# First half of the experts' down product as three rounded products, and gathered rows in two buffers in place of four

## The reference

```python
def swiglu(x, w_gate, w_up, w_down):
    return (jax.nn.silu(x @ w_gate) * (x @ w_up)) @ w_down
...
    def block(args):
        tok, e = args
        return swiglu(h_pad[tok], w_gate[e], w_up[e], w_down[e])

    out = lax.map(block, (row_tok.reshape(n_blocks, MOE_BLOCK), blk_exp))
    out = out.reshape(n_rows, D) * row_w[:, None]
    return jax.ops.segment_sum(out, row_tok, num_segments=T + 1)[:T]
```

## Time and profile before

| | |
|---|---|
| median of 3 runs | 2048.01 us (2043.39 to 2048.45) |
| the profiled execution | 2049.21 us, span 2047.6 us |
| PE busy | 1928.1 us, 94% of the span |
| DVE busy | 1038.1 us, 51% |
| ACT busy | 874.1 us, 43% |
| POOL busy | 373.5 us, 18% |
| mean rate of all transfers | 195 GB/s over the span |

### The profile page before, as it was taken

One profiled execution on the slowest core, in us unless ns is written; L12 is line 12 of the kernel. 1 busy time (PEld: TensorE's weight loads), 2 busy tenths in 40 slices (PEclk: granted clock), 3 DMA queues, 4 the chain that ended last, 5 costly groups with the idle time before them and its releaser, 6 DMA issues. The chain is left out here.

```text
span 2047.6 us, 34503 instructions
## 1 busy us (share of the span) xinstructions
PE 1928.1 (94%) x10264; PEld 1495.0 (73%) x10265; DVE 1038.1 (51%) x1532; ACT 874.1 (43%) x1210; POOL 373.5 (18%) x337
## 2 busy tenths in 40 slices
PE   4999999899899999989789999999999999999995
PEld 3999999899788666755547777777777777777772
DVE  4113401166438335545426666666666666666665
ACT  5110111244212212221246666666666666666663
POOL 0100100111111000000212222232223222222220
PEclk9999999899899999999889999999999999999997
DMA  7211311111443665425069896999998888897964
GB/s 260 74 52 41 123 52 31 32 63 62 144 142 113 229 230 206 143 85 196 1 228 347 261 346 182 317 295 300 331 301 271 269 273 306 244 352 253 300 180 172
DMA packets 182101, 399.64 MB, mean 195 GB/s; under 512 B 22425, under 2 KB 87185, under 8 KB 182046
## 3 DMA queue, kind: packets, MB, share of 16 engines
q1 hardware_dynamic: 149166, 312.16, 42.5%
q0 software_dynamic: 31680, 82.49, 15.7%
q10 hardware_dynamic: 1200, 4.26, 0.6%
HBM read 351.27 MB, written 80.64 MB: 211 GB/s over the span
## 5 line engine op out<-in xcount | busy, mean ns | idle before, releaser
L2184 DVE TENSOR_TENSOR wexp_lo<-wexp,wexp_hi 128x2048 fp32r<-128x2048 f32 x190 | 426.9, 2288 | 91.3 <-ACT wexp_hi L2135 88.3
L2135 ACT ACTIVATE wexp_hi<-wexp 128x2048 fp32r x190 | 353.4, 1907 | 52.4 <-issue 49.4
L2111 PE MATMUL bank<-wexp_down,hTe 128*128 x736 | 330.6, 592 | 0.0
L2086 PE MATMUL bank<-wexp_hi,x_hi 128*128 128x512 f32 x744 | 300.5, 404 | 3.8 <-DVE wexp_lo L2184 3.8
L2086 PE MATMUL bank<-wexp_hi,x_lo 128*128 128x512 f32 x744 | 292.0, 393 | 0.0
L2086 PE MATMUL bank<-wexp_lo,x_hi 128*128 128x512 f32 x744 | 290.4, 390 | 0.0
L2059 POOL DMA_INDIRECT acc_d<-ob,ixs x92 | 153.7, 1670 | 615.8 <-DMA acc_d<-ob,ixs 441.9
L2111 PEld LDWEIGHTS bank<-wexp_down,hTe 128*128 128x128 f32 x736 | 139.1, 189 | 139.4 <-issue 132.3
L547 PE MATMUL bank<-hT_hi,w_hi 128*128 128x344 f32 x576 | 187.3, 325 | 7.3 <-DVEq L659 7.3
L547 PE MATMUL bank<-hT_hi,w_lo 128*128 128x344 f32 x576 | 185.1, 321 | 0.0
L547 PE MATMUL bank<-hT_lo,w_hi 128*128 128x344 f32 x576 | 184.6, 320 | 0.0
(11 more groups left out here) (357 smaller groups left out, 2988.7 us busy)
## 6 DMA issues: line engine op xcount, KB each, us to landing
wexp<-in_w_exp_gate SPq DMA_DIRECT2D x128, 512.0 KB
wexp<-in_w_exp_up SPq DMA_DIRECT2D x128, 512.0 KB
wexp_down<-in_w_exp_down SPq DMA_DIRECT2D x128, 512.0 KB
wada<-in_w_ada SPq DMA_DIRECT2D x12, 2048.0 KB, 10.9
w_raw<-in_w_in SPq DMA_DIRECT2D x44, 512.0 KB, 3.9
gates_d<-gst POOLq DMA_DIRECT2D x48, 172.0 KB, 2.1
gate<-gates_d SPq DMA_DIRECT2D x16, 516.0 KB, 5.8
xn<-in_x_prompt ACTq DMA_DIRECT2D x8, 512.0 KB, 8.3
```

What stands on the lines that cost most here:

```text
L2086: last = pe.matmul(banks[0][:].rearrange("p (g n) -> p g n", g=2), stat[:, b, k, :], mov[:, b, :, k * FF:(k + 1) * FF], start=(k == 0 and ...
L2111: last = pe.matmul(banks[4 + half][:], hT[:, f, :], wdn[:, bass.ds(slot, 1), f, half * 512:half * 512 + 512].rearrange("p a n -> p (a n)") ...
L2135: act.activation(w_hi[:, b, g, :], wexp[:, bass.ds(e & (RING - 1), 1), g, :].rearrange("p a n -> p (a n)"), ACT.Copy).then_inc(whi_ok, 1)
L2184: dve.tensor_tensor(w_lo[:, b, g, :], wexp[:, bass.ds(e & (RING - 1), 1), g, :].rearrange("p a n -> p (a n)"), w_hi[:, b, g, :], ALU.subtr ...
```

## The change

Of the down product the first half of the contraction (the transposed `hh`'s first 128 rows, `h0`, and the expert's first 128 rows of down weights, `d0`) is now computed as three fp32r products; the second half (`h1`) stays float32. For it ACT rounds `h0` and `d0`, and DVE makes their rests. The `d0` work of block i+1 is put between the two halves of the gate and up weights' work of block i+3; on DVE the second half of that work moves over the block boundary into the next block's start. The gathered rows have two buffers in place of four, and a gather runs four blocks ahead in place of six. `hh` shares the buffer of `sg`.

```diff
-AHEAD = 6
+AHEAD = 4
+ROOMS = 2
...
-            xg = nc.alloc_sbuf_tensor_at("xg", [P, RING, XW], F32, offset=at)
+            xg = nc.alloc_sbuf_tensor_at("xg", [P, ROOMS, XW], F32, offset=at)
...
-        hh = tile("hh", [P, FF])
-        hT = tile("hTe", [P, FF // P, P])
+        hh = sg
+        h0_hi = tile("hTe_hi", [P, P], F32R)
+        h0_lo = tile("hTe_lo", [P, P], F32R)
+        h1 = tile("hTe_1", [P, P])
+        d0_hi = tile("down_hi", [P, D], F32R)
+        d0_lo = tile("down_lo", [P, D], F32R)
...
                     sp.wait_ge(dn_ps, before)
+                    sp.wait_ge(dlo_ok, before)
                     load_down(sp, a, wdn, expert_at(part, g), slot, down_in)
...
                 def block_of(i, q):
                     b = q % 2
                     pool.wait_ge(x_tp, i + 3)
                     pool.wait_ge(wc_ok, i + 3)
+                    pool.wait_ge(ix_ok, i + 1)
+                    pool.sem_inc(passed, 1)
                     gather(i + AHEAD, (q + AHEAD) % RING)
...
-                    pe.wait_ge(hT_ok, i + 1)
                     pe.wait_ge(ob_ok, 2 * i + 2)
+                    pe.wait_ge(h0lo_ok, i + 1)
+                    pe.wait_ge(dlo_ok, i + 1)
+                    for half in range(2):
+                        for n, (stat, mov) in enumerate(((h0_hi, d0_hi), (h0_hi, d0_lo), (h0_lo, d0_hi))):
+                            last = pe.matmul(banks[4 + half][:], stat[:], mov[:, half * 512:half * 512 + 512], start=(n == 0),
+                                             stop=False)
+                    last.then_inc(d0_ps, 1)
+                    pe.wait_ge(h1_ok, i + 1)
                     pe.wait_ge(down_in, e * 32 + 32)
                     for half in range(2):
-                        for f in range(FF // P):
-                            last = pe.matmul(banks[4 + half][:], hT[:, f, :],
-                                             wdn[:, bass.ds(slot, 1), f, half * 512:half * 512 + 512].rearrange("p a n -> p (a n)"),
-                                             start=(f == 0), stop=(f == FF // P - 1))
+                        last = pe.matmul(banks[4 + half][:], h1[:],
+                                         wdn[:, bass.ds(slot, 1), 1, half * 512:half * 512 + 512].rearrange("p a n -> p (a n)"),
+                                         start=False, stop=True)
                     last.then_inc(dn_ps, 1)
...
+                def round_down(j):
+                    e = entry(act, j, 1, E - 1)
+                    act.wait_ge(down_in, e * 32 + 32)
+                    if j is not 0:
+                        act.wait_ge(d0_ps, j)
+                    act.sem_inc(passed, 1)
+                    act.activation(d0_hi[:], down_first(e), ACT.Copy).then_inc(dhi_ok, 1)
...
                     act.wait_ge(h_tp, i + 1)
-                    act.activation(hT[:].rearrange("p f n -> p (f n)"), banks[3][:, 0:FF], ACT.Copy).then_inc(hT_ok, 1)
+                    act.activation(h1[:], banks[3][:, P:FF], ACT.Copy).then_inc(h1_ok, 1)
+                    act.activation(h0_hi[:], banks[3][:, 0:P], ACT.Copy).then_inc(h0hi_ok, 1)
                     take(i + 2, b)
                     gate(i + 1)
-                    round_weights(i + 3, 1 - b)
+                    round_weights(i + 3, 1 - b, lambda: round_down(i + 1))
                     act.wait_ge(dn_ps, i + 1)
...
+                def rest_of_down(e, j):
+                    dve.wait_ge(dhi_ok, j + 1)
+                    dve.tensor_tensor(d0_lo[:], down_first(e), d0_hi[:], ALU.subtract).then_inc(dlo_ok, 1)
+
+                def turned(j):
+                    dve.wait_ge(h0hi_ok, j + 1)
+                    dve.tensor_tensor(h0_lo[:], banks[3][:, 0:P], h0_hi[:], ALU.subtract).then_inc(h0lo_ok, 1)
...
                 def block_of(i, q):
                     b = q % 2
+                    rest_of_weights(entry(dve, i + 2, 1, E - 1), i + 2, b, 1)
+                    turned(i)
                     take(i + 2, b)
                     to_gather(i + AHEAD, (q + AHEAD) % RING)
                     gate(i + 1)
...
                     weight(e, (q + 3) % RING, gathered(i, q, 3))
-                    rest_of_weights(e, i + 3, 1 - b)
+                    rest_of_weights(e, i + 3, 1 - b, 0)
+                    rest_of_down(entry(dve, i + 1, 1, E - 1), i + 1)
```

More of the change, by code:

```diff
@@ L1902, in tile @@
             return sb(name, shape, dt, ctx)
[L1904 removed]
+        tile("xg_room", [P, ROOMS, XW])
         x_hi = tile("x_hi", [P, 2, KD, P], F32R)
@@ L1917, in experts @@
         ixs = [tile(f"ixs{b}", [P, 1], U32) for b in range(2)]
-        names = "ix ixs tp xhi xlo wc whi wlo gu sg h hp hT dn ob scat wu wd pad".split()
-        (ix_ok, ixs_ok, x_tp, xhi_ok, xlo_ok, wc_ok, whi_ok, wlo_ok, gu_ps, sg_ok, h_ok, h_tp, hT_ok, dn_ps, ob_ok, added,
-         up_ok, _, pad_ok) = (sem("s6" + n) for n in names)
+        names = "ix ixs tp xhi xlo wc whi wlo gu sg h hp h0hi h0lo h1 dhi dlo d0 dn ob scat wu pad".split()
+        (ix_ok, ixs_ok, x_tp, xhi_ok, xlo_ok, wc_ok, whi_ok, wlo_ok, gu_ps, sg_ok, h_ok, h_tp, h0hi_ok, h0lo_ok, h1_ok, dhi_ok,
+         dlo_ok, d0_ps, dn_ps, ob_ok, added, up_ok, pad_ok) = (sem("s6" + n) for n in names)
         passed = sem("s6passed")
@@ L1946, in experts, with down_first @@
         last = Final(nc, a, o, sem, banks, ident, eps, wexp, acc_d, kept_in, w_at)
+        def down_first(e):
+            return wdn[:, bass.ds(e & (RING - 1), 1), 0, :].rearrange("p a n -> p (a n)")
         def gathered(i, q, ahead):
@@ L2013, in _ @@
                 n = blocks_done(sp)
-                sp.wait_ge(wlo_ok, n * 2 + 6)
+                sp.wait_ge(wlo_ok, n * 2 + 5)
                 sp.sem_inc(ended, 1)
@@ L2025, in _ @@
             def _(pool):
[L2026 to L2029, removed]
                 pool.memset(none[:], 0.0).then_inc(pad_ok, 1)
@@ L2038, in gather @@
                 def gather(j, q):
-                    pool.wait_ge(ix_ok, j - (RING - 1))
-                    pool.sem_inc(passed, 1)
-                    pool.indirect_dma_start(out=xg[:, q, 0:XW], out_offset=None, in_=xe_d,
+                    pool.indirect_dma_start(out=xg[:, q % ROOMS, 0:XW], out_offset=None, in_=xe_d,
                                             in_offset=bass.IndirectOffsetOnAxis(ap=ix[q][:, 0:1], axis=0),
                                             bounds_check=LAST_ROW, oob_is_err=False).then_inc(gat[q], 16)
[L2045 to L2048, removed]
+                for j in range(ROOMS, AHEAD):
+                    pool.wait_ge(x_tp, j - 1)
+                    pool.wait_ge(wc_ok, j - 1)
+                    gather(j, j)
                 def block_of(i, q):
@@ L2076, in turn @@
                     for k in range(KD):
-                        last = pe.transpose(banks[1 + k // 4][:, (k % 4) * P:(k % 4 + 1) * P], xg[:, q, k * P:(k + 1) * P],
+                        last = pe.transpose(banks[1 + k // 4][:, (k % 4) * P:(k % 4 + 1) * P], xg[:, q % ROOMS, k * P:(k + 1) * P],
                                             ident[:])
@@ L2117, in _ @@
                 n = blocks_done(pe)
-                pe.wait_ge(wlo_ok, n * 2 + 6)
+                pe.wait_ge(wlo_ok, n * 2 + 5)
                 pe.wait_ge(ob_ok, n * 2 + 2)
@@ L2134, in round_weights @@
                     for g in range(2):
+                        if g and amid:
+                            amid()
                         act.activation(w_hi[:, b, g, :],
@@ L2148, in _ @@
                 round_weights(2, 0)
+                round_down(0)
                 def block_of(i, q):
@@ L2178, in weight, with rest_of_weights @@
                     dve.sem_inc(passed, 1)
-                    dve.tensor_copy(wcol[:, q:q + 1], xg[:, q, bass.ds(e + D, 1)]).then_inc(wc_ok, 1)
-                def rest_of_weights(e, j, b):
-                    for g in range(2):
-                        dve.wait_ge(whi_ok, 2 * j + g + 1)
-                        dve.tensor_tensor(w_lo[:, b, g, :],
-                                          wexp[:, bass.ds(e & (RING - 1), 1), g, :].rearrange("p a n -> p (a n)"),
-                                          w_hi[:, b, g, :], ALU.subtract).then_inc(wlo_ok, 1)
+                    dve.tensor_copy(wcol[:, q:q + 1], xg[:, q % ROOMS, bass.ds(e + D, 1)]).then_inc(wc_ok, 1)
+                def rest_of_weights(e, j, b, g):
+                    dve.wait_ge(whi_ok, 2 * j + g + 1)
+                    dve.tensor_tensor(w_lo[:, b, g, :],
+                                      wexp[:, bass.ds(e & (RING - 1), 1), g, :].rearrange("p a n -> p (a n)"),
+                                      w_hi[:, b, g, :], ALU.subtract).then_inc(wlo_ok, 1)
+                def rest_of_down(e, j):
[4 more added lines that the diff above has]
+                    dve.tensor_tensor(h0_lo[:], banks[3][:, 0:P], h0_hi[:], ALU.subtract).then_inc(h0lo_ok, 1)
                 def gate(j):
@@ L2200, in _ @@
                 take(0, 0)
-                to_gather(4, 0)
-                rest_of_weights(e, 0, 0)
```

(6 more changed lines are left out.)

5 lines of the change are left out of this document (3 added, 2 removed).

## The result

The changed kernel takes **2062.64 us** (median of 7 runs, 2056.54 to 2067.6) against 2048.45 (7 runs, 2043.39 to 2050.18) for the kernel before. The ratio is 1.0074, with a 95% interval of 1.0055 to 1.0092: 0.7% slower, where 0.7% faster was forecast. The profiled execution is the one of 2062.64 us, with a span of 2061.0.

The account below looks back on a forecast made before the run. PE was taken to set the pace, transfers close behind. From 2048.0 us, -31.5 (PE), +12 (down loads), +3 (two buffers) and +2 (ends) made -14.5, so 2033.5; forecast range 2024 to 2042, 8-in-10 range 2017 to 2060.

Parts of the forecast that it names:

- PE saves 0.34 a block, period 9.68: Down product on PE: two float32 matmuls become six fp32r ones, 31.5 us less over 92 blocks.
- ACT and DVE fit: Added rounding stays hidden: ACT's round 8.35 under 9.68; DVE's `hTe_lo` at 6.05 against PE's need at 6.59.
- The 0.5 us to spare: DVE's margin for `hTe_lo` before PE needs it; named as where the prediction fails most easily.
- The look-up of 0.49: ACT's look-up of the expert's number ahead of `down_hi`: 0.49 where uncovered, here covered by the first `wexp_hi`.
- The down load, +12: `down_hi` needs down weights 6.7 sooner than PE did; dense runs lose 12 us together, between 0 and 20.
- The two buffers, +3: Gathers behind scatters on POOL, rows needed two blocks later instead of four: 3 us lost, between 0 and 13.
- The scatters' own interval: POOL's chain of scatters, each waiting for the one before to land; kept at 10.02 only by PE's pace.
- slower: Rival, chance 0.21: chain scatter, gather, `wcol`, `wexp_lo`, `hTe_lo` becomes the bound; 10.15 in all blocks, 2062 us.
- The ends, +2: First block's `hTe_lo` 1 us later and last `ob` 1 us later behind `down_hi`: 2 us.
- The rule of the Trainium skill: Two-input DVE work and GpSimd instructions reading SBUF exclude each other; a gather so hit costs 1.7, left out of the sum.

Follow-up runs that it names:

- e6: Changed kernel with SP's down loads moved one expert earlier: 2056.56 us, ratio 1.0051.
- e1: Kernel before, float32 down product kept, with only the gathered rows' two buffers and the gather four blocks ahead: 2051.84 us, ratio 1.0017.
- e3: Changed kernel with `down_hi` and `down_lo` made for the first block alone and used by all: 2045.89 us, ratio 0.9990.
- e8: Changed kernel with `hTe_lo` before the second half of `wexp_lo`, gather issued ahead of the scatter, down loads one expert earlier: 2043.72 us, ratio 0.9979.
- e10: e8's kernel with scatters that overwrite instead of adding: 2020.84 us, ratio 0.9874.
- e4: Changed kernel with scatters that overwrite instead of adding: 2039.18 us, ratio 0.9959.
- e2: Changed kernel with the gather of the block five ahead issued before the block's scatter on POOL: 2057.51 us, ratio 1.0054.
- e5: Changed kernel with `hTe_lo` made before the second half of `wexp_lo` on DVE: 2061.41 us, ratio 1.0070.

## Why the prediction was wrong

**PE saves 0.34 a block, period 9.68:** right, 9.67 in the chain.

**ACT and DVE fit:** right where nothing is late. In the block from 1374.18, `ob` ends at 3.82 (3.92 forecast) and `hTe_lo` at 5.97 (6.05):

```profile
1374.18 0.39 PE L2107 MATMUL bank<-ident,sg 128*128 128x128 f32 x2
...
1376.76 1.24 ACT L2185 ACTIVATE ob<-bank,wcol 128x512 f32<-128x512 f32 x2
...
1379.87 0.28 DVE L2217 TENSOR_TENSOR hTe_lo<-bank,hTe_hi 128x128 fp32r<-128x128 f32 x1
```

The 0.5 us to spare was right, and I named it as the weak place. What the step left out is the turn of a loop. DVE's costs 2.25 to 2.36 ahead of the second half of `wexp_lo` in three places (1083.88, 1247.12, 1491.31), and at PE's the transposes come 4.1 to 5.2 after the end of `hTe_lo` where they are late. Both were hidden before, so the trace showed neither.

**The look-up of 0.49:** right, nothing waits for it.

**The down load, +12:** right place, half the size. ACT waits 14.9 us in 9 blocks ahead of `down_hi` (12 forecast), and e6 gives back 6, with intervals that overlap. But in block 16 above this load and the loop's turn came together, so the term can't be cut out alone.

**The two buffers, +3:** e1 measures them at 3.9, at the old pace.

**The scatters' own interval, put at nothing in the sum: the step that failed.** The working says that only PE's pace, not the chain's own, has kept the scatters at 10.02, and prices no more than the lag of single gathers behind them. A scatter lands 9.2 us after its issue (median, e3 and e8), and the next can't start before. The profile's chain has scatters of 9.01, 11.18, 9.65 and 9.40 us, begun 9.88, 12.06 and 10.51 apart:

```profile
1482.90 9.01 DMA acc_d<-ob,ixs
1492.78 11.18 DMA acc_d<-ob,ixs
1504.84 9.65 DMA acc_d<-ob,ixs
1515.35 9.40 DMA acc_d<-ob,ixs
```

So in such a stretch the chain's own interval is above 9.66. Over the stage e8 gives an estimate of it: 86 of its 92 scatters stood behind a landing, directly or by way of `ixs`, and its intervals after the first have a mean of 9.90. I had written that 77 waits behind a landing cost PE nothing today. True; but POOL waiting for landings in 77 blocks out of 92 says that the chain has little slack at 10.02, some 0.1 by e8, and 0.35 was to be taken from it.

Taken in the order e8, e10, the medians divide the loss of 47 us so: 19 for the three late inputs, against 17 forecast for the loads, the buffers and the ends; 23 for the scatters' landing, against nothing forecast; some 5 are left. In another order the shares may differ.

The rival that I called *slower* names this chain, at a chance of 0.21, and it gave 2062. Its mechanism held in part: the scatters' landing costs 23 us (e4, e10), while the look-up's wait for a gather (e2) was worth 5 by itself. Its condition, a mean interval of the scatters above 10.02, is met (10.13, from 1094.7 to 1976.3 with 88 scatters), but shows nothing by itself: every block has one scatter, so whatever delays the blocks lengthens it. And that its number is met is in part luck: it took 10.15 for every block, where half of them took PE's 9.66 or little more and the first took 15.33.

**The ends, +2:** the first block alone lost 5.7; the stage's first transposes come 1.2 later and the end is 1.6 shorter than before, 5 in all.

**The rule of the Trainium skill** (SBUF — State Buffer, on the shared port pair) agrees with the trace: the scatter at 1247.25, issued into DVE's `wexp_lo`, took 3.62 us against a usual 1.58 and ended 1.46 after it, and the mean rose from 1670 to 1798 ns. It is not what decides: in e4 scatters took POOL 1927 ns on average, longer still, and the kernel was 23 us faster.

What stays open: how the late inputs' share divides among loop turns, gathers and loads in the changed kernel. They cover one another (e5 to e8), and no run separates them all. Four buffers with the rounded products were not tried.

## What to carry to other kernels

A wait that costs nothing today is a second bound: before work is taken from the engine that sets the pace, work out the own period of every chain beside it (here landing plus the next issue, 9.9 us against 9.66), since the gain ends there. Put a product's last-made operand as early on its engine as its inputs allow, and look at what a loop's turn does to it: slack that is enough in a block of straight code was not enough there. When several late inputs meet at one engine, removing one may show nothing; try them together before calling one innocent.

## What was not expected of the hardware

- A stall can cost more than its length, and not every one does. After 3.97 us of idle PE the granted clock was 0.60 over the next 3.5 us, and the 512-column products came 0.43 us apart in place of 0.23. After 2.26 us idle (at 1249.71) it was 0.51, near the lower of the two levels (1.2 GHz; 1.00 is 2.4). After 2.23 us idle (at 1493.90) it stayed at 1.00:

```profile
1249.70:1253.00 3.30, 3.29 (x7) 2.43 (x8) 3.30 (x7) 0.76 (x2) 2.42 (x2) 0.51 0.53 60
1493.90:1497.40 3.50, 3.50 (x14) 2.30 (x14) 3.50 (x7) 0.60 (x1) 2.62 (x2) 1.00 0.75 195
```

The two slowed stretches cost 1.4 + 1.6 = 3 us.

- Where PE's loop turned and its next transposes were late, they came 4.1 to 5.2 us after the end of `hTe_lo`, the last input that PE waited for (9 places), and 3.7 to 5.0 in e4 (17 places).
- A scatter of 128 rows of 1024 that adds lands in 9.2 us at the median (e3, e8), one that overwrites in 7.9 (e4).
